# Second norm moved into the linear attention, a split modulation and a rotation by transfers in a two-block fp32 kernel

## The reference, cut to what matters

```
# first block
mod = silu(c) @ ada_w + ada_b;  shift, scale, gate = split(mod, 3)
h = rmsnorm(x, norm_g) * (1 + scale) + shift
y = gla_mixer(h, ...)                 # chunked gated linear attention, 4 heads
h1 = rmsnorm(x + gate * y, final_g)
# second block
mod = silu(c_2) @ w_mod_2 + b_mod_2   # and once more for c_ctx_2, the context
u  = rms_norm(h1,  norm_w_2) * (1 + scale) + shift
uc = rms_norm(ctx, norm_w_2) * (1 + scale_c) + shift_c
p = u @ w_in_2                        # q, k, v, gates, conv input: 22 column tiles of 128
k_c, v_c = kv of uc @ w_in_2[:, k and v columns]
q, k = rope_2d(norm per head of q and k)
# then attention over context and own keys, a 31 wide depthwise conv, the output product
```

## Time and profile before

| | us |
|---|---|
| median of 3 runs | 2878.21 (2877.74 to 2882.36) |
| the profiled execution | 2884.46 |
| its span, first to last instruction | 2882.7 |
| TensorE busy in it | 2605.2 (90%), mean granted clock 0.952 |
| DVE busy | 1672.5 (58%) |
| ACT busy | 1044.2 (36%) |
| POOL busy | 765.5 (27%) |

### The profile page before, as it was taken

The page is one execution under the profiler, slowest core; times in us unless marked ns, Lnnn a source line. Parts: engine busy times, 40 slices in busy tenths (PEclk is TensorE's granted clock), DMA queues, the critical chain, the costliest instruction groups (busy, mean ns, idle before and its releaser), DMA issues. The chain is left out here.

```text
span 2882.7 us, 35232 instructions
## 1 busy us (share of the span) xinstructions
PE 2605.2 (90%) x11685; PEld 1754.7 (61%) x11685; DVE 1672.5 (58%) x2673; ACT 1044.2 (36%) x1830; POOL 765.5 (27%) x359
## 2 busy tenths in 40 slices
PE   8599899999999995699999993999999999947997
PEld 1177677777777774577777761444445544525776
DVE  0106542541542352488989866677777777746564
ACT  0234343343343331431313121445444444433332
POOL 0034321101111100003030112565556666631000
PEclk9799999999999997899999996899999999978999
DMA  8366578377567634557575654011111111033334
GB/s 318 106 220 196 184 246 287 126 251 257 189 215 249 215 126 159 194 182 261 186 252 185 225 177 101 23 28 29 32 29 28 28 28 28 24 121 114 120 131 146
DMA packets 233927, 433.54 MB, mean 150 GB/s; under 512 B 20513, under 2 KB 112151, under 8 KB 233552
## 3 DMA queue, kind: packets, MB, share of 16 engines
q1 hardware_dynamic: 207524, 337.48, 35.3%
q10 hardware_dynamic: 26284, 94.51, 9.5%
HBM read 326.77 MB, written 96.76 MB: 147 GB/s over the span
## 5 line engine op out<-in xcount | busy, mean ns | idle before, releaser
L1726 DVE TENSOR_REDUCE att_mx<-att_bank_m 128x1 f32<-128x512 f32 (+1 forms) x640 | 365.2, 629 | 114.1 <-PE att_bank_m L1590 110.3
L1694 ACT ACTIVATE att_p_f<-att_bank_s 128x512 f32<-128x512 f32 x576 | 317.9, 598 | 289.8 <-PE att_bank_s L1631 283.6
L456 PE MATMUL gla_bank_g<-gla_a_hi,gla_w_hi 128*128 128x512 f32 x1024 | 415.9, 406 | 5.2 <-POOL gla_w_lo L409 4.3
L456 PE MATMUL gla_bank_g<-gla_a_hi,gla_w_lo 128*128 128x512 f32 x1024 | 403.9, 394 | 0.0
L456 PE MATMUL gla_bank_g<-gla_a_lo,gla_w_hi 128*128 128x512 f32 x1024 | 403.5, 394 | 0.0
L1575 POOL TENSOR_TENSOR att_den<-att_den,att_p_f 128x1024 f32<-128x1024 f32 x160 | 378.9, 2368 | 36.3 <-ACT att_p_f L1694 24.2
L1342 DVE SCALAR_TENSOR_TENSOR proj_conv_acc<-proj_conv_in,proj_conv_w,proj_conv_acc 128x512 f32<-128x512 f32 (+1 forms) x480 | 353.1, 805 | 0.0
L1152 PE MATMUL proj_bank_g<-proj_u_hi,proj_w_hi 128*128 128x512 f32 x704 | 287.1, 408 | 3.7 <-DVE proj_u_lo L1330 3.7
L1152 PE MATMUL proj_bank_g<-proj_u_lo,proj_w_hi 128*128 128x512 f32 x704 | 274.3, 390 | 0.0
L1152 PE MATMUL proj_bank_g<-proj_u_hi,proj_w_lo 128*128 128x512 f32 x704 | 274.2, 389 | 0.0
L1605 PE MATMUL att_bank_o<-att_p_f,att_v 128*64 128x512 f32 x1152 | 270.1, 604 | 0.0
(11 more groups left out here) (325 smaller groups left out, 4032.5 us busy)
## 6 DMA issues: line engine op xcount, KB each, us to landing
gla_w_hi<-scratch_w_hi SPq DMA_DIRECT2D x96, 512.0 KB, 4.2
gla_w_lo<-scratch_w_lo SPq DMA_DIRECT2D x96, 512.0 KB, 5.6
proj_w_hi<-scratch_w_hi ACTq DMA_DIRECT2D x90, 512.0 KB, 3.8
proj_w_lo<-scratch_w_lo ACTq DMA_DIRECT2D x90, 512.0 KB, 4.7
scratch_w_hi<-gla_w_hi SPq DMA_DIRECT2D x54, 512.0 KB, 4.4
scratch_w_lo<-gla_w_lo SPq DMA_DIRECT2D x54, 512.0 KB, 5.5
mod_wslab<-in_ada_w SPq DMA_DIRECT2D x6, 2048.0 KB, 11.3
mod_wslab<-in_w_mod SPq DMA_DIRECT2D x6, 2048.0 KB, 8.0
```

What stands on the lines that cost most here:

```text
L456: last = pe.matmul(banks[s % 2][:], w[:, k, :], a[:, k, :], start=(k == 0 and n == 0), stop=(k == KT - 1 and n == 2))
L1694: act.activation(p_f[:, kt, :], S[kt % SBANKS][:], ACT.Exp, scale=float(HD) ** -0.5).then_inc(p_done, 1)
L1726: dve.reduce_max(mx[:, qt, n:n + 1], M[p % MBANKS][:, 0:min(TB, KEYS - TB * n)], AX_X).then_inc(mx_read, 1)
```

## The change

- `modulation` works off `ada_w` only. The 8 products of a slab go to four groups of PSUM partitions (0, 32, 64, 96), two products each; ACT copies four parts, and a product with a constant `group_sum` adds the groups and turns the row. x is loaded behind the slabs, squared on ACT and scaled on DVE in this phase; the first raw weights and constants of `gla_block` are loaded here too.
- `gla_block` works off `w_mod_2` in block 0: `modulate(j)` behind turn j for j from 0 to 5, slabs on ACT's queue into two places, DVE copies the parts, `turn_row` follows a turn later. In blocks 1 to 3 the second norm of the block before follows the first (`square_h1`, `root_of_h`, `round_u`, `split_u`), and u is stored in two parts.
- The last block's x1 stays in SBUF; its two norms are worked off in blocks 1 and 2 of `projections`. The high and low activations and the weight ring keep their places from one phase to the next, and SP loads the first u and four weight pairs at the end of `gla_block`.
- In `projections` blocks 0 to 2 read u; the context is worked on within block 0 (turns 2 to 18). The rotation's partner comes from eight transfers of 16 partitions (`swap_q`), the sign is in the sin table. The spread is one fp32r product with both parts of the factor in its rows. `TAPS_OF_TURN` has 4 carried taps a turn instead of 8.

```diff
-                for n in range(2 * NS):
-                    w = d["ada_w"] if n < NS else d["w_mod_2"]
+                for n in range(NS):
                     if n >= SLOTS:
                         sp.wait_ge(slab_used, UP + n - SLOTS + 1)
-                    sp.dma_start(wslab[n % SLOTS][:], w.rearrange("(k p) n -> p k n", p=P)[:, :, WC * (n % NS):WC * (n % NS + 1)]
+                    sp.dma_start(wslab[n % SLOTS][:], d["ada_w"].rearrange("(k p) n -> p k n", p=P)[:, :, WC * n:WC * (n + 1)]
                                  ).then_inc(slab_landed[n % SLOTS], 16)
+                sp.dma_start(x_tok, d["x"].rearrange("(t p) n -> p t n", p=P)[:, 0:NT, :]).then_inc(x_landed, 16)
+                w_in = d["gla_w_in"].rearrange("(k p) n -> p k n", p=P)
+                for n in range(2):
+                    sp.dma_start(keep["w_raw"][n][:], w_in[:, :, P * n:P * (n + 1)]).then_inc(keep["w_landed"][n], 16)
+                sp.dma_start(keep["glr_raw"][:], w_in[:, :, GLA_VEND:GLA_VEND + RANK]).then_inc(keep["consts"], 16)
+                for name, src in (("sel", "sel"), ("reset", "reset"), ("ones", "ones"), ("w_alpha", "gla_w_alpha")):
+                    sp.dma_start(keep[name][:], d[src]).then_inc(keep["consts"], 16)
...
+                act.wait_ge(parts_clear, UP + 1)
+                for n in range(NS):
                     act.wait_ge(slab_used, UP + n + 1)
-                    act.activation(rows[m][:, WC * (n % NS):WC * (n % NS + 1)], bank[n % 2][0:1 + m, :], ACT.Copy).then_inc(row_copied, 1)
+                    for g in range(GROUPS):
+                        part = slice(GROUP_GAP * g, GROUP_GAP * g + 1)
+                        act.activation(rows[part, WC * n:WC * (n + 1)], bank[n % 2][part, :], ACT.Copy).then_inc(row_copied, 1)
+                act.wait_ge(x_landed, UP + 16)
+                for t in range(NT):
+                    if t:
+                        act.wait_ge(x_squared, UP + t)
+                    act.activation(unread[:], x_tok[:, t, :], ACT.Square, accum_out=x_st[:, 0, t:t + 1]).then_inc(x_squared, 1)
...
                     for k in range(KT):
-                        lhs = csil[:, k:k + 1] if m == 0 else csil[:].rearrange("p (v k) -> p k v", k=8)[:, k, 1:3]
-                        last = pe.matmul(bank[n % 2][0:1 + m, :], lhs, wslab[n % SLOTS][:, k, :], start=(k == 0), stop=(k == KT - 1))
+                        g = k % GROUPS
+                        last = pe.matmul(bank[n % 2][GROUP_GAP * g:GROUP_GAP * g + 1, :], csil[:, k:k + 1], wslab[n % SLOTS][:, k, :],
+                                         start=(k < GROUPS), stop=(k >= KT - GROUPS))
                     last.then_inc(slab_used, 1)
-                    if n == NS:
-                        turn_rows(0, ps_mod1)
-                turn_rows(1, ps_mod2)
+                pe.wait_ge(group_sum_landed, UP + 16)
+                pe.wait_ge(row_copied, UP + GROUPS * NS)
+                for j in range(3 * KT):
+                    pe.matmul(ps_mod[:, j:j + 1], rows[:, P * j:P * (j + 1)], group_sum[:, 0:1], start=True, stop=True)
...
+                dve.wait_ge(x_squared, UP + NT)
+                dve.tensor_scalar(x_st[:, 1, :], x_st[:, 0, :], 1.0 / D, EPS, ALU.mult, ALU.add).then_inc(x_mean, 1)
+                dve.wait_ge(x_mean, UP + 1)
+                small_rsqrt(dve, x_st[:, 2, :], x_st[:, 1, :], x_st[:, 3, :], x_step, 0)
+                dve.wait_ge(x_step, UP + SMALL_STEPS)
+                for t in range(NT):
+                    dve.tensor_scalar(x_tok[:, t, :], x_tok[:, t, :], x_st[:, 2, t:t + 1], None, ALU.mult).then_inc(x_scaled, 1)
...
+                def store_u(b):
+                    sp.wait_ge(u_lo_made, UP + b * 8 + 8)
+                    for part, src in (("u_hi", o_t), ("u_lo", xr)):
+                        sp.dma_start(u_of[part][:, :, ds(b * TB, TB)], src[:]).then_inc(u_stored, 16)
...
+                def load_early_u():
+                    for half in range(2):
+                        chunks = slice(4 * half, 4 * half + 4)
+                        for part, dst in (("u_hi", a_hi), ("u_lo", a_lo)):
+                            sp.dma_start(dst[:, chunks, :].bitcast(F32), u_of[part][:, chunks, 0:TB]).then_inc(u_early[half], 16)
...
+                        if j == 9 and b:
+                            store_u(b - 1)
...
+                sp.wait_ge(proj, UP + NB * NW - 2)
+                load_early_pair(2)
+                sp.wait_ge(proj, UP + NB * NW - 1)
+                load_early_pair(0)
+                sp.wait_ge(proj, UP + NB * NW)
+                load_early_u()
+                load_early_pair(1)
...
+                def modulate(n):
+
+                    pe.wait_ge(slab_landed[n % 2], UP + 16 * (n // 2) + 16)
+                    pe.wait_ge(row_copied, UP + GROUPS * n)
+                    for k in range(KT):
+                        g = k % GROUPS
+                        last = pe.matmul(mod_bank[GROUP_GAP * g:GROUP_GAP * g + 2, :], csil[:].rearrange("p (v k) -> p k v", k=KT)[:, k, 1:3],
+                                         wslab[n % 2][:, k, :], start=(k < GROUPS), stop=(k >= KT - GROUPS))
+                    last.then_inc(slab_used, 1)
+
+                def turn_row(n):
+                    pe.wait_ge(row_copied, UP + GROUPS * (n + 1))
+                    for i in range(WC // P):
+                        last = pe.matmul(mod_at[:, 4 * n + i, :], mod_row[n % 2][:, P * i:P * (i + 1)], group_sum[:], start=True, stop=True)
+                    last.then_inc(row_turned, 1)
...
+                            j = 4 * g + s
+                            if b == 0 and 1 <= j <= NS:
+                                turn_row(j - 1)
+                            if b == 0 and j < NS:
+                                modulate(j)
...
+                        if b == 0 and 1 <= j < NS - 1:
+                            act.wait_ge(slab_used, UP + j)
+                            load_slab(j + 1)
+                        if b:
+                            if j == 0:
+                                rsqrt_x1(b - 1)
+                            if j in (1, 2):
+                                for c in range(4 * (j - 1), 4 * j):
+                                    square_h1(b - 1, c)
+                            if j == 4:
+                                root_of_h(b - 1)
+                            if j in (5, 6):
+                                for c in range(4 * (j - 5), 4 * (j - 4)):
+                                    round_u(b - 1, c)
...
+                def split_u(b):
+
+                    for c in range(1, KT):
+                        add_h1_squares(b, c)
+                    dve.wait_ge(u_sum, UP + b + 1)
+                    dve.wait_ge(ot_copied, UP + b * 8 + 8)
+                    dve.tensor_scalar(u_mean, O[:, 0, :], 1.0 / D, EPS, ALU.mult, ALU.add).then_inc(u_ms, 1)
+                    dve.wait_ge(u_rs0, UP + b + 1)
+                    newton_rsqrt(dve, u_root, u_mean, xr[:, 3, :], u_step, b * 4)
+                    dve.wait_ge(u_step, UP + b * 4 + 4)
+
+                    def rest_of_u(c):
+                        dve.wait_ge(u_hi_made, UP + b * 8 + c + 1)
+                        dve.scalar_tensor_tensor(xr[:, c, :].bitcast(F32R), xr[:, c, :], modv[:, 1, c:c + 1], o_t[:, c, :],
+                                                 ALU.add, ALU.subtract).then_inc(u_lo_made, 1)
+                    for c in range(KT):
+                        dve.scalar_tensor_tensor(xr[:, c, :], o_t[:, c, :], gains[:, 1, c:c + 1], u_root, ALU.mult, ALU.mult).then_inc(u_scaled, 1)
+                        if c:
+                            rest_of_u(c - 1)
+                    rest_of_u(KT - 1)
+
...
+                def copy_row(n):
+                    dve.wait_ge(slab_used, UP + n + 1)
+                    dve.wait_ge(glr_split, UP + 2)
+                    dve.wait_ge(row_turned, UP + max(n - 1, 0))
+                    for g in range(GROUPS):
+                        part = slice(GROUP_GAP * g, GROUP_GAP * g + 2)
+                        dve.tensor_copy(mod_row[n % 2][part, :], mod_bank[part, :]).then_inc(row_copied, 1)
+                for n in range(NS):
+                    copy_row(n)
...
-    TAPS_OF_TURN = [8] * 4 + [8] + [7] * 6 + [4, 5, 5, 2, 4, 4, 3, 3, 4, 4, 4]
+    TAPS_OF_TURN = [4] * 4 + [8] + [7] * 9 + [4, 5, 4, 5, 4, 5, 5, 5]
...
+                def swap_q(b, i):
+
+                    n = b * 5 + i
+                    sp.wait_ge(q_n, UP + n + 1)
+                    if n >= 2:
+                        sp.wait_ge(q_done, UP + n - 1)
+                    for g in range(0, P, 32):
+                        for to, of in ((g, g + 16), (g + 16, g)):
+                            sp.dma_start(qsin[to:to + 16, n % 2, :], qraw[of:of + 16, i, :]).then_inc(q_swapped[n % 2], 16)
...
+                        if j == 14 and b == 0:
+                            sp.wait_ge(cv_done, UP + 1)
+                            load_u(1)
+                        if j == 1 and b == 1:
```

(43 more changed lines are left out.)

562 lines of the change are left out of this document (314 added, 248 removed).

## The result

The changed kernel takes 2796.5 us (median of four runs, 2790.5 to 2803.2) against 2880.1 (four runs, 2877.7 to 2882.4): ratio 0.9711, 95% interval 0.9685 to 0.9736, 83.5 us or 2.9% faster. The forecast was 2750 with a range of 2728 to 2788: the direction is right, the time lies 8.5 us above the range and the gain is 45 us smaller than forecast. The profiled execution took 2790.5 us, the quickest of the four, against 2884.5 before, so the traces differ by 94.0 us and have 34 us of the shortfall to explain.

The account below looks back on a forecast made before the run. TensorE was taken to bound linear attention and projections, with four other stretches totalling 257 us; 70 - 26 - 8 + 52 + 36 - 6 + 10 = 128 us gained gives 2756 profiled, 2750 median, range 2728 to 2788.

Parts of the forecast that it names:

- Head: Way to the linear attention: grouped slab products let transfers set the pace; 70 us gained, bounds 60 and 73.
- 4 us (bounds 1.6 and 10...): Head: the 24 sums over column groups take 4 us in all and hide behind the x work.
- Block 0: Linear attention's first block: working off the second modulation matrix there loses 26 us, bounds 13 and 44.
- Blocks 1 to 3: Linear attention's later blocks: the second norm there loses 8 us, bounds 0 and 20.
- 2 us a block: Blocks 1 to 3: u's stores on SP delay turn 12's weights, 6 us in all, plus 2 for the clock.
- Change of phase: Linear attention to projections: turn 1 starts 62 us earlier; less 9.5 of work moved into block 0, 52 gained.
- Projections: Projection stage: 36 us gained from less TensorE work, 6 lost to DVE; 9.5 of moved work also falls here.
- (2.14 - 0.33) x 20 = 36: Projections: dropping the rotation and a one-pass spread save TensorE 36 us over 20 turns, bounds 30 and 38.
- Rival (c): Projections: DVE or the swap becomes the bound, half of the 36 unseen, block 2 costs 12; 2774 us, chance 0.12.
- Tail: Behind the last z: 21 taps and a product with sin instead of 36 taps; 10 us gained.
- (b): Linear attention: transfers hurt more, block 0 costs 40 and the norms 20; 2776 us, chance 0.14.
- rival (a): Head and block 0: the column groups don't run together; 2787 us, chance 0.13.

Follow-up runs that it names:

- e9: Changed kernel with x loaded before the head's last two slabs, its norm worked off early and group sums taken slab by slab: 2785.0 us.
- e6: Changed kernel with DVE working off the norm of x before it forms the modulation's columns: 2792.5 us.
- e7: Changed kernel loading only the first two slabs of the second modulation matrix in block 0 and using them for all six (result wrong): 2786.8 us.
- e2: Changed kernel with the low part of u stored at turn 11, not right behind the high part at turn 9: 2782.6 us.
- e8: Changed kernel with ACT copying the first product of the projections before its context work: 2795.2 us.
- e12: Changed kernel with DVE's step that norms a query one turn earlier, ahead of that turn's z and taps: 2786.5 us.
- e13: Changed kernel with the three changes of e10 and the earlier norming step of e12: 2757.2 us, ratio 0.9568 to the kernel before.
- e10: Changed kernel with the changes of e9, e2 and e8 together: 2767.9 us, ratio 0.9602 to the kernel before.
- e11: Changed kernel without GpSimd's two steps of the rotation, the product with cos and the sum: 2778.5 us.
- e1: Changed kernel with all eight slab products of both modulation matrices in one column group, one copy a slab instead of four: 2829.6 us.

## Why the prediction was right in direction and too large

- **Head, 70 forecast, 64.9 measured.** Groups, transfer rate and the time of the last slab were right. The failed step is that the sums take "4 us (bounds 1.6 and 10...)" and "hide behind the x work": they took 9.56, near the upper bound, at a clock that fell to half (four take 1.05 us at the full clock in e9, so 24 would be 6.3), and the last 4.2 us of them were not hidden, because on DVE x's norm stood behind them; e6 gets 3.8 back. I had checked the cover by time, not by the order on the engine.
- **Block 0, -26 forecast, -25.3 measured.** Right for a wrong reason: I took 22 us of late slabs, 1 of sums and 3 of clock. By e7 it is 15 of products and sums (by their lengths 17) and 10.5 of waits with the clock behind them. The products were left out of most turns since I thought them hidden in waits that mostly weren't there.
- **Blocks 1 to 3, -8 forecast, -20.2 measured; the largest miss.** The mechanism, weights of turn 12 behind u on SP, was the forecast's own; its size was off. "2 us a block" was 3.1 to 4.4 of wait, 5 to 7 with the clock behind it, since an issue behind 2 MB stores takes 3 to 4 us itself. The row that told it, 1.63 us for one constant's issue, I used only for the phase change. The sum of squares, 1.0 us of TensorE a block, I didn't count. e2 shows 17.8 of the 20.2 to be that queue order.
- **Change of phase, 62 forecast, 56.3 measured.** The new phase starts 10.0 us behind the last result, where 9.3 was forecast. "ACT's context prelude ends about 1139, just before turn 2 needs it" failed: two banks mean that turn 2 needs the copy of product 0, which stood behind that prelude; e8 gives 5.5 back.
- **Projections, 20.5 forecast, 9.4 measured.** The step "(2.14 - 0.33) x 20 = 36" is nearly right about TensorE's work (between the two copies it is busy for 22.7 us less, with some 9.5 of context work moved in, so 32 of the 36) and wrong about who sets the pace. I weighed DVE by its work in a block, 134 us against 129, and gave it 6. Block 2 came out so, 133.2; but block 1 took 133.9, and block 3 131.0, which loses as many spreads and rotations from 135.9 and would be at 127. The ring of spread, norming step, z and taps binds in each of those turns, also in blocks where DVE has time to spare. e12 gives 8.6 us back in three blocks by order alone (and loses 2.4 in block 2), and e13 is 10.7 us shorter than e10. Rival (c) named DVE or the swap; it was DVE, and in three of the four blocks not by capacity.
- **Tail, 10 forecast, 4.6 measured.** 21 taps and sin at 0.68 are right for an idle GpSimd; beside its last steps they took 18.1 us (5.48, 0.68 and 11.95), and DVE reached the last z 2.8 us behind ACT's copy, where it was 1.2 before. e11 priced GpSimd's part at 3.9.
- **Attention and output.** 4.2 us came there that the change doesn't touch, spread over the stage. I have no cause for them; the kernel before's profiled execution was 4.4 us above its median, which may be the same 4 us, but that isn't shown.

The rivals were priced as alternatives, and two happened together: the norms at 20 of (b), and (c) in part. These are 12 and 11 us, and the head, the phase change and the tail add 16: 39 us short, less 5 that came where none was forecast (block 0 and the last stage), 34. So the terms alone put the median at 2784, near the high end of the range and inside it. The other 12 us that bring it to 2796.5 are the 10.5 between traces and medians and 2 that the kernel before's median rose with its fourth run. The 6 of them on the changed kernel's side I put down to the projections' single long turns, which come and go between runs of the same code; that is argued from the spread of the table, not shown. That the time lies above the range, and not just inside it, is therefore partly bad luck; that the traces' gain is a quarter smaller than forecast is not.

Slips in the working: x's norm before took 10.3 us by the rows, not 10.1; the weights of turn 12 come out 19.2 us behind turn 8's end, not 19.6; rival (a)'s 57 is 18 us behind 38.9, not 19. None moves the forecast by more than 1 us.

## What to carry to other kernels

When work is taken off the bounding engine, follow each handover on its path (bank, buffer, copy) to where the releasing instruction stands on its own engine: DVE, busy for 85% of the stage, set the pace of turn after turn here, and one instruction moved ahead of five others gave 6 us in that stage, and 10.7 in all once other changes had brought the work ahead of it forward. Check that cover is there in the order of the engine, not only in time, and price an issue behind megabyte stores at its backed-up length. A wait of TensorE of about 3 us mostly cost another 2 us or more in low clock here, though not every time, so small waits are worth removing one by one, and rivals that can happen together should be added.

## What the runs showed of the hardware

- Four column groups of one or two columns run fully together: 8 fp32 products of 512 columns in 1.90 us, and 7.03 in one group (e1).
- Sums over groups with one result column and 98 rows took 0.40 us each while the clock fell to half (24 in 9.56, mean clock 0.55) and 0.26 at the full (4 in 1.05), so a row of them isn't cheap for its size. The row stood behind a wait of 2.6 us; the clock was at 1.00 in that wait and at 0.50 from 2.3 us into the row to its end, though TensorE shows no gap of more than 0.1 us in it.
- A wait of TensorE of 2.9 us was followed by 6 us at 0.50 to 0.62 of the clock (e10_all), one of 3.3 by 4 us at 0.60 (changed kernel). One of 3.4 us was followed by 6 us at 1.00 in two kernels and at 0.72 in six others. A wait of 1.1 us in the projections left it at 1.00.
- An issue on SP right behind a 2 MB store took 3.2 to 4.4 us, each of the swap's small ones 0.6 to 0.9 in the mean of eight, 1.2 once.
